# Activation operands of the 256-token stages at 1024 bytes from k-tile to k-tile instead of 1088

## What is computed

```python
def swiglu(h, w_gu, w_down):
    g, u = jnp.split(h @ w_gu, 2, axis=-1)
    return (jax.nn.silu(g) * u) @ w_down

# first_block, for layers i = 0 and 1
f = swiglu(rms_norm(h, ln_ffn1[i, 0]), ffn1_w_gu[i], ffn1_w_down[i])
h = h + 0.5 * rms_norm(f, ln_ffn1[i, 1])
hn = rms_norm(h, ln_mix[i, 0])
# i = 0: short convolution mixer; i = 1: differential attention mixer, 8 heads
h = h + rms_norm(m, ln_mix[i, 1])
f = swiglu(rms_norm(h, ln_ffn2[i, 0]), ffn2_w_gu[i], ffn2_w_down[i])
h = h + 0.5 * rms_norm(f, ln_ffn2[i, 1])
# second_block, on the 256 tokens that are left
mod = silu(c) @ w_mod + b_mod                      # six vectors of 1024
proj = (rms_norm(x) * (1 + sc_m) + sh_m) @ w_in    # q, k, v of two attentions, index, gates
merged = sigmoid(gate_a) * (o_a @ w_br_dsa) + sigmoid(gate_b) * (o_b @ w_br_moba)
x = x + gt_m * (merged @ w_out)
x = x + gt_f * swiglu(rms_norm(x) * (1 + sc_f) + sh_f, w_gate_up, w_down)
```

## The kernel before, in words

| tensor | address | modulo 256 | step per k-tile |
|---|---|---|---|
| `w_hi`, `w_lo` | 111552, 144320 | 192, 192 | tiles of 512 bytes |
| `x_hi`, `x_lo` | 185792, 194496 | 192, 192 | 1088 |
| `a_hi`, `a_lo` | 16512, 40448 | 128, 0 | 1088 |
| `o2_hi`, `o2_lo` | 16512, 24704 | 128, 128 | 1024 |
| `z_hi`, `z_lo` | 32896, 41088 | 128, 128 | 1024 |

## Time and profile before

### The profile page before, as it was taken

How to read it: one execution, slowest core, us unless ns; L and a number is a source line. 1 busy time by engine, 2 the same in 40 slices (tenths; PEclk the granted TensorE clock), 3 DMA queues, 4 the chain that set the end, 5 groups by cost and what they waited for, 6 DMA issues and landing times. The chain is left out here.

```text
span 1598.5 us, 28870 instructions
## 1 busy us (share of the span) xinstructions
PE 1517.6 (95%) x11846; PEld 1479.7 (93%) x11846; DVE 1060.0 (66%) x1415; ACT 684.2 (43%) x806; POOL 14.6 (1%) x31
## 2 busy tenths in 40 slices
PE   5999989989999899998999889999789999989999
PEld 5999989989999899998988689999788989989999
DVE  5666787766667856667755557667768665686653
ACT  5434352364343543434445354443433435454431
POOL 0000000000000000000000000000000000000000
PEclk9999989989999999999999799999799999999999
DMA  8454655534546455555422126456533324445450
GB/s 312 168 186 173 241 182 188 183 125 172 185 172 247 177 186 184 181 211 217 152 81 104 53 80 224 172 205 222 190 132 121 117 107 158 159 158 197 172 204 33
DMA packets 38155, 269.11 MB, mean 168 GB/s; under 512 B 4240, under 2 KB 5392, under 8 KB 5680
## 3 DMA queue, kind: packets, MB, share of 16 engines
q1 hardware_dynamic: 33120, 240.31, 41.8%
q0 software_dynamic: 3792, 26.44, 4.7%
q10 hardware_dynamic: 1152, 1.05, 0.2%
HBM read 266.73 MB, written 1.05 MB: 168 GB/s over the span
## 5 line engine op out<-in xcount | busy, mean ns | idle before, releaser
L327 PE MATMUL ps<-x_hi,w_hi 128*128 128x272 f32 (+1 forms) x2512 | 740.3, 295 | 44.0 <-DVE w_lo L864 15.2
L328 PE MATMUL ps<-x_lo,w_hi 128*128 128x272 f32 (+1 forms) x2512 | 727.2, 290 | 0.0
L329 PE MATMUL ps<-x_hi,w_lo 128*128 128x272 f32 (+1 forms) x2512 | 725.6, 289 | 0.0
L1599 ACT ACTIVATE w_hi<-raw_weights 128x2048 fp32r<-128x2048 f32 x228 | 434.8, 1911 | 382.9 <-PE ps L329 378.2
L864 DVE TENSOR_TENSOR w_lo<-raw_weights,w_hi 128x2048 fp32r<-128x2048 f32 x194 | 442.3, 2290 | 167.4 <-ACT w_hi L1599 167.2
L327 PEld LDWEIGHTS ps<-x_hi,w_hi 128*128 128x128 f32 x2512 | 485.2, 193 | 51.8 <-issue 30.0
L328 PEld LDWEIGHTS ps<-x_lo,w_hi 128*128 128x128 f32 x2512 | 484.9, 193 | 2.8 <-issue 2.4
L329 PEld LDWEIGHTS ps<-x_hi,w_lo 128*128 128x128 f32 x2512 | 484.0, 193 | 0.0
L327 PE MATMUL ps<-a_hi,w_hi 128*128 128x272 f32 (+1 forms) x1008 | 289.1, 287 | 2.1 <-DVE w_lo L864 1.9
L329 PE MATMUL ps<-a_hi,w_lo 128*128 128x272 f32 (+1 forms) x1008 | 288.3, 286 | 0.0
L328 PE MATMUL ps<-a_lo,w_hi 128*128 128x272 f32 (+1 forms) x1008 | 288.2, 286 | 0.0
(11 more groups left out here) (209 smaller groups left out, 1038.5 us busy)
## 6 DMA issues: line engine op xcount, KB each, us to landing
raw_weights<-w_units SPq DMA_DIRECT2D x228, 1024.0 KB, 4.9
mod_w<-mod_units POOLq DMA_DIRECT2D x24, 1024.0 KB, 5.3
h<-x_in SPq DMA_DIRECT2D x1, 1088.0 KB, 5.1
out<-h ACTq DMA_DIRECT2D x8, 128.0 KB, 1.8
con<-constants POOLq DMA_DIRECT2D x1, 592.0 KB, 8.4
tab<-tables POOLq DMA_DIRECT2D x1, 512.0 KB, 3.5
f<-constants POOLq DMA_DIRECT2D x1, 136.0 KB, 8.5
vec<-vectors SPq DMA_DIRECT2D x1, 100.5 KB, 2.1
```

What stands on the lines that cost most here:

```text
L327: pe.matmul(dst, wh, hi, start=start, stop=False)
L328: pe.matmul(dst, wh, lo, start=False, stop=False)
L329: return pe.matmul(dst, wl, hi, start=False, stop=stop)
L1599: act.activation(w_hi[:, u % RING, :], raw[:, u % RING, :], ACT.Copy).then_inc(S["hi_ready"], 1)
```

## The change

New tensors for 256 tokens are laid over the old ones, and all 256-token stages use them. `x_hi_s` starts where `x_hi` starts (185792), `x_lo_s` 8192 bytes on (193984); `a_hi_s` starts where `a_hi` starts (16512), `a_lo_s` 24576 bytes on (41088). Modulo 256, x starts at 192 for every k-tile and a at 128 for every k-tile, high and low part alike. The tensor `v1` of the attention moves by 128 bytes. The 272-token stages keep their tensors. Instructions, their order, their sizes and their waits stay as they are.

```diff
         a_hi = at("a_hi", 0, [P, FT, TOK], F32R)
         a_lo = at("a_lo", a_bytes, [P, FT, TOK], F32R)
+        a_hi_s = at("a_hi_s", 0, [P, FT, SEQ], F32R)
+        a_lo_s = at("a_lo_s", 24 * 1024, [P, FT, SEQ], F32R)
+        a_of = {TOK: (a_hi, a_lo), SEQ: (a_hi_s, a_lo_s)}
...
-        free1, free2 = 8 * TOK * 4, a_bytes + 8 * TOK * 4
+        free1, free2 = 8 * TOK * 4, 32 * 1024
...
+        x_at = -(-nc.sbuf_base // 32) * 32
         x_hi = sb("x_hi", [P, KT, TOK], F32R)
         x_lo = sb("x_lo", [P, KT, TOK], F32R)
+        x_hi_s = nc.alloc_sbuf_tensor_at("x_hi_s", [P, KT, SEQ], F32R, offset=x_at)
+        x_lo_s = nc.alloc_sbuf_tensor_at("x_lo_s", [P, KT, SEQ], F32R, offset=x_at + KT * SEQ * 4)
+        x_of = {TOK: (x_hi, x_lo), SEQ: (x_hi_s, x_lo_s)}
...
-                group(st, 0, (x_hi, x_lo), x_base=x_base, between=between)
+                group(st, 0, x_of[st.T], x_base=x_base, between=between)
...
-            k_outer(stages["down", 4], (a_hi, a_lo), A0["up", 4])
+            k_outer(stages["down", 4], a_of[SEQ], A0["up", 4])
...
-                dve.tensor_tensor(a_lo[:, k, 0:T], up, a_hi[:, k, 0:T].bitcast(F32), ALU.subtract).then_inc(S["a_ready"], 2)
+                hi, lo = a_of[T]
+                dve.tensor_tensor(lo[:, k, 0:T], up, hi[:, k, 0:T].bitcast(F32), ALU.subtract).then_inc(S["a_ready"], 2)
```

More of the change, by code:

```diff
@@ L471, in first_groups @@
                 c.up("rstd_kept")
-                group(st, 1, (x_hi, x_lo), bank_busy=lambda m: wait_side(part, m))
+                group(st, 1, x_of[st.T], bank_busy=lambda m: wait_side(part, m))
             def gate_up(n, x_base, part=None, deferred=True):
@@ L478, in gate_up @@
                 else:
-                    group(st, 0, (x_hi, x_lo), x_base=x_base)
-                    group(st, 1, (x_hi, x_lo), bank_busy=lambda m: wait_side(part, m))
+                    group(st, 0, x_of[st.T], x_base=x_base)
+                    group(st, 1, x_of[st.T], bank_busy=lambda m: wait_side(part, m))
                 with pe.Fori(0, 4) as i:
-                    group(st, 2, (x_hi, x_lo), i)
-                    group(st, 3, (x_hi, x_lo), i)
-                group(st, 10, (x_hi, x_lo))
+                    group(st, 2, x_of[st.T], i)
+                    group(st, 3, x_of[st.T], i)
+                group(st, 10, x_of[st.T])
             gate_up(0, 0)
@@ L648, in _ @@
             early = [m for m in range(8) if attn_out.bank(attn_out.t0 + m) < 4]
-            a_in = (a_hi, a_lo)
+            a_in = a_of[SEQ]
             def early_slab(k):
@@ L677, in _ @@
             gate_up(3, X0["up", 3])
-            k_outer(stages["down", 3], (a_hi, a_lo), A0["up", 3])
+            k_outer(stages["down", 3], a_of[SEQ], A0["up", 3])
             w_in = stages["w_in"]
@@ L693, in small_group @@
                             wait_bank(w_in, w_in.t0 + m)
-                        ins = three_pass(ps[:, m, 0:SEQ], u % RING, (k * 2 + m) * P, x_hi[:, k, 0:SEQ],
-                                         x_lo[:, k, 0:SEQ], k == 0, k == KT - 1)
+                        ins = three_pass(ps[:, m, 0:SEQ], u % RING, (k * 2 + m) * P, x_hi_s[:, k, :],
+                                         x_lo_s[:, k, :], k == 0, k == KT - 1)
                         if k == KT - 1:
@@ L814, in _ @@
             small_group()
+            xs = x_of[SEQ]
             group(w_in, 0, xs, between={1: [lambda: key_and_weights()]})
@@ L1026, in update_and_prepare @@
                 deferred = shift is None
+                hi, lo = x_of[T]
                 for m in range(8 + 2):
@@ L1049, in update_and_prepare @@
                             dve.wait_ge(S["x_hi_ready"], c.up("x_hi_ready"))
-                            dve.scalar_tensor_tensor(x_lo[:, k, 0:T], h[:, k, off:off + T], next_gain[:, k:k + 1],
-                                                     x_hi[:, k, 0:T].bitcast(F32), ALU.mult, ALU.subtract)\
+                            dve.scalar_tensor_tensor(lo[:, k, 0:T], h[:, k, off:off + T], next_gain[:, k:k + 1],
+                                                     hi[:, k, 0:T].bitcast(F32), ALU.mult, ALU.subtract)\
                                .then_inc(S["x_ready"], 1)
@@ L1080, in update_and_prepare @@
                         dve.wait_ge(S["x_hi_ready"], c.up("x_hi_ready"))
-                        dve.tensor_tensor(x_lo[:, k, 0:T], f[:, k, 0:T], x_hi[:, k, 0:T].bitcast(F32),
+                        dve.tensor_tensor(lo[:, k, 0:T], f[:, k, 0:T], hi[:, k, 0:T].bitcast(F32),
                                           ALU.subtract).then_inc(S["x_ready"], 1)
@@ L1255, in subln_lo @@
                 dve.wait_ge(S["a_hi_ready"], E0["qkv"] + r + 1)
-                dve.tensor_tensor(a_lo[:, heads, 0:SEQ], o1[:, heads, :], a_hi[:, heads, 0:SEQ].bitcast(F32),
+                dve.tensor_tensor(a_lo_s[:, heads, :], o1[:, heads, :], a_hi_s[:, heads, :].bitcast(F32),
                                   ALU.subtract).then_inc(S["a_ready"], 2)
@@ L1611, in gated @@
                 act.wait_ge(S["act_in_ready"], I0["up", n] + g + 1 + 2 * i)
-                act.activation(a_hi[:, bass.ds(2 * g + 4 * i, 2), 0:T], pair_b[:, :, 0:T], ACT.Copy)\
+                act.activation(a_of[T][0][:, bass.ds(2 * g + 4 * i, 2), 0:T], pair_b[:, :, 0:T], ACT.Copy)\
                    .then_inc(S["a_hi_ready"], 1)
@@ L1664, in prepare @@
                     if not full:
-                        act.activation(x_hi[:, m, 0:T], h[:, m, off:off + T], ACT.Identity,
+                        act.activation(x_of[T][0][:, m, 0:T], h[:, m, off:off + T], ACT.Identity,
                                        scale=next_gain[:, m:m + 1]).then_inc(S["x_hi_ready"], 1)
@@ L1674, in prepare @@
                         act.wait_ge(S["full_ready"], c.up("full_ready"))
-                        act.activation(x_hi[:, m, 0:T], f[:, m, 0:T], ACT.Copy).then_inc(S["x_hi_ready"], 1)
+                        act.activation(x_of[T][0][:, m, 0:T], f[:, m, 0:T], ACT.Copy).then_inc(S["x_hi_ready"], 1)
             def before_evictions(nx, bank):
@@ L1767, in subln_hi @@
                 act.wait_ge(S["act_in_ready"], I0["qkv"] + r + 1)
-                act.activation(a_hi[:, heads, 0:SEQ], o1[:, heads, :], ACT.Copy).then_inc(S["a_hi_ready"], 1)
+                act.activation(a_hi_s[:, heads, :], o1[:, heads, :], ACT.Copy).then_inc(S["a_hi_ready"], 1)
             def split():
```

## The result

The changed kernel takes 1605.8 us (median of 12 runs, 1600.91 to 1609.59) and the kernel before 1601.43 us (median of 12 runs of the same series, 1596.91 to 1605.49): a ratio of 1.003, 95% interval 1.0018 to 1.0041, that is 2.9 to 6.6 us slower. In a second series of 12 runs against 23 the ratio was 1.0022 (1.0013 to 1.0031). Forecast was +3.2 us, a ratio of 1.002, and a time of 1606.4 us. The profiled execution has a span of 1602.6 us and took 1604.41 us, so that 1.8 us lie around the span; before it was 1598.5.

What follows compares the result with a forecast made beforehand. TensorE's matmul spacing, set by addresses, was taken as the bound in most 256-token stages. x +6.4 and a -3.2 gave +3.2 us on the median 1603.15, so 1606.4 us, range 1598 to 1612.

Steps and rivals of the forecast that it cites:

- The spacing follows the distance to the weights: 256-token matmuls: spacing depends on the moving operand's start against the weights' start modulo 256; 120 ns at 192 against 192.
- x, +6.4: Up 3, up 4 and w_in: dense x at an even 120 ns costs 2.4, 2.4 and 1.6 us (sum 5.7 to 7.3).
- Down 4, -2.5: Down 4: dense a at 128 runs at 113.3 ns in place of 118.0, gaining 2.5 us over 528 matmuls.
- Attn_out, -0.7: Attn_out: 192 matmuls on the dense a, some broken up by attention's small ones, gain 0.7 us (0 to 0.9).
- z's pattern: The slower of two steady patterns at 128 against the weights' 192, seen in stage z: 117.7 ns per matmul.
- rival 1: Down 4 and attn_out: a keeps a spacing near 118 ns, its term about -0.1, total 1609.4 us; chance 0.18.
- Down 3, 0: Down 3: no gain; bound by modulation units, its wait for low weights grows from 2.1 to about 4.5 us.
- o2's pattern: The quicker of two steady patterns at 128 against the weights' 192, seen in stage o2: 113.1 ns per matmul.
- Rival 5: Whole kernel: the change does nothing, spacings come from what else runs beside TensorE; 1603 us; chance 0.05.
- Rival 3: Up 3, up 4, w_in: dense x runs at 113.3 ns since hi, lo and k-tiles stand alike; -16, 1587 us; chance 0.12.

Runs made afterwards that it cites:

- x at 128: The changed kernel with the dense x 192 bytes later, starting at 128 modulo 256; 1591.15 us against 1600.55 for the kernel before, ratio 0.994.
- the weights at 128: The changed kernel with 192 bytes put ahead of the weight ring, moving weights and dense x to 128 modulo 256; 1611.42 us against 1600.55, ratio 1.007.
- x alone: Only x made dense, a and `v1` keeping their old places; 1607.78 us against 1600.55 for the kernel before, ratio 1.0043.
- second profile of before: The kernel before, unchanged, profiled once more, for w_in; 1606.76 us in its one profiled run.
- a alone: Only a made dense, x keeping its step of 1088; 1598.73 us against 1600.55 for the kernel before, ratio 0.9995.
- the change again: The changed kernel, unchanged, run once more for a second profile; 1605.34 us against 1601.93 for the kernel before.
- x at 0: The changed kernel with the dense x 64 bytes later, starting at 0 modulo 256; ratio 1.0002 to the kernel before.
- x at 96: The changed kernel with the dense x 160 bytes later, starting at 96 modulo 256; ratio 0.9977 to the kernel before.

## Why the prediction was right

- **The spacing follows the distance to the weights.** Right for the 256-token stages, and shown from both sides: by moving x (up 4 at 113.4 ns with x at 128, 120.0 in the change) and by moving the weights under a resting a (down 4 at 113.4 ns in the change, 120.0 with the weights at 128). The forecast for the dense x, an even 120 ns, was exact. Why the distance matters, no run shows.
- **The time, 1606.4 us against 1605.8.** That these lie 0.6 us apart is in part luck. The forecast was built on a median of three runs, 1603.15 us, and twelve runs give 1601.43, 1.7 us less; the change itself was put at +3.2 us and is +4.4. The two misses cancel in part.
- **x, +6.4.** Up 3 and up 4 were put at +2.4 each; they show +2.25 and +1.80, and +2.4 in x alone, where the low-clock share was that of before. W_in was put at 1.6, with 2.5 as the upper end. The profile shows +4.56, of which about 2.0 are left at equal low-clock time; the rest lies with 7.3 us more at the low clock, an amount by which two executions of the kernel before differ as well. The term was a little small, and the end was passed by something that the prediction had not reckoned with at all.
- **Down 4, -2.5.** Measured -2.43, 113.4 ns in the whole stage.
- **Attn_out, -0.7.** Measured -0.12. After its pauses it fell into z's pattern (117.2 ns on the mean). This was within the bounds, and it is the part of rival 1 that came true. In this stage, with TensorE's waits in it, the pattern could not be counted on: of nine profiles with this a at 128 and the weights at 192, four have 114 ns in attn_out and five 117 to 118.
- **Down 3, 0.** The profile shows -2.5, which looks like a refutation. But with the old a it also took 63.83 us in x alone, at full clock, against 65.88 in the first and 66.97 in the second profile of before, both with 3.4 us at the low clock. At equal clock the new a is worth 63.83 - 63.37 = 0.5 us, or 0.2 to 0.7 by the other profiles at full clock (63.64 in a alone, 63.13 in the change again). The matmuls' 2.5 us went where it was said, into the wait for the low part of the weights:

```profile
PEld ps L334 <- DVE w_lo L872: 3.4, 2, 2.3
```
```profile
PEld ps L332 <- DVE w_lo L870: 1.6, 1, 1.6
```

The first row is of the waits in the changed kernel and answers to the earlier trace rows: 3.4 us where 2.1 were; 4.5 were forecast. The chain of modulation units ran 0.8 us quicker in this execution (VectorE comes to that w_lo 55.6 us after the stage's first matmul in place of 56.4), which accounts for most of what is missing. The second row is of x alone, the kernel with the old a at full clock. Against it the wait is 1.8 us longer and the stage 0.5 us shorter, which makes up the 2.4 us that the matmuls gain. A single wait proves less: in the second profile of before it is 3.4 us as well.

- **What was not foreseen.** The branch products went from o2's pattern to the slower one, +0.84 us, with no change of their own operands. In the second profile of the change they were back at 21.75 us. It is chance of the same kind as in attn_out.
- **Rival 5**, the layout is not the cause. The measurement decides against it: with nothing but the start of x moved, up 4 runs at 113.4 ns (x at 128) or at 120.0 (the change), and with the weights at 128 down 4, whose a did not move, runs at 120.0 ns in place of 113.4.
- **Rival 3** asked the right question, whether the dense step can be as quick as o2's. It can, at another start: x at 128. Its own cause, that high and low part stand alike, is refuted by the change itself, where they do and x runs at 120.0 ns.

## What to carry to other kernels

Where TensorE is the bound and every matmul loads its own weights, look at the spacing of starts by k-tile, not at a mean over the stage: in up 4 of the kernel before the k-tiles run at 115.4 to 118.6 ns on the mean, and here it came from addresses. Before a layout is made regular, find which of the remainders it will freeze: here the mixed step of 1088 gave 117.6 ns in up 4, and the even step of 1024 gave 113.4, 117.3, 117.8, 118.3 or 120.0 ns for the whole stage, by its start. Here 192 bytes of offset turned +0.3% into -0.6%.

## What the runs showed that I had not expected

- Two steady patterns at one and the same placement (128 against 192): 113.3 and 117.8 ns, for a whole stage of 528 matmuls (down 4 behind x at 128 and behind x at 0). Which one sets in differs between stages and between profiles of one kernel (o2 has 117.8 and 113.4 ns in the two profiles of the change); no rule that the runs bear out foretells it (down 3 and down 4 of x at 96 run at 117.8 and 113.4 ns behind x at 117.4 and 117.3 ns).
- In w_in the time at the low clock, 0.50 of full speed, differs between the two profiles of the kernel before by 9.5 us (10.1 and 19.6), and w_in by 3.3 us (192.65 and 195.94). A stage difference of that size in two single profiles is no evidence by itself, down 3's included.
- At 272 columns the start at 128 is worth 2.0 ns per matmul in up 1 against the mixture of starts. At 256 columns the same comparison gives 4.3 ns (117.6 to 113.3 in up 4), and the worst start against the best 6.6 ns. Other even starts were not tried at 272 columns.
